# First MLP's down projection: three of its four groups by seven half-tile products per two-by-two block instead of eight

## The reference, cut to what matters

```python
def squared_relu_mlp(x, w1, w2):
    return jnp.square(jax.nn.relu(x @ w1)) @ w2

# in first_block, layer i = 0:
f = squared_relu_mlp(rms_norm(h, pre_mlp_norm[i]), w_mlp_in[i], w_mlp_out[i])
h = h + rms_norm(f, post_mlp_norm[i])
```

## Time and profile before

| quantity | value |
|---|---|
| median of three runs | 2287.64 us |
| span of the profiled execution | 2286.1 us |
| PE busy | 2252.4 us (99% of the span), 10594 matmuls |
| PEld busy | 1848.7 us (81%) |
| POOL busy | 1577.5 us (69%) |
| DVE busy | 1267.0 us (55%) |
| ACT busy | 657.5 us (29%) |
| mean granted clock of PE | 0.997 of full speed |
| DMA | 202.35 MB, mean 89 GB/s |

### The profile page before, as it was taken

How to read it: one execution, slowest core, us unless ns; L and a number is a source line. 1 busy time by engine, 2 the same in 40 slices (tenths; PEclk the granted TensorE clock), 3 DMA queues, 4 the chain that set the end, 5 groups by cost and what they waited for, 6 DMA issues and landing times.

```text
span 2286.1 us, 27986 instructions
## 1 busy us (share of the span) xinstructions
PE 2252.4 (99%) x10594; PEld 1848.7 (81%) x10594; DVE 1267.0 (55%) x1852; ACT 657.5 (29%) x1201; POOL 1577.5 (69%) x1534
## 2 busy tenths in 40 slices
PE   8999999999999999999999999999999999999998
PEld 6888888888888788888888888888677788888887
DVE  7774746335345777175554364368865445626354
ACT  3443432101013455154221011142464233202113
POOL 8666568777777455644597777779445938878784
PEclk9999999999999999999999999999999999999999
DMA  5222233333333111211243333324222413333332
GB/s 168 87 73 85 70 92 92 102 100 98 96 97 89 55 39 40 76 42 53 78 118 108 97 108 104 97 84 142 82 65 70 124 52 97 97 98 97 97 95 77
DMA packets 114264, 202.35 MB, mean 89 GB/s; under 512 B 13009, under 2 KB 21713, under 8 KB 114129
## 3 DMA queue, kind: packets, MB, share of 16 engines
q1 hardware_dynamic: 109424, 194.67, 29.3%
q10 hardware_dynamic: 4704, 5.89, 0.8%
HBM read 196.19 MB, written 2.10 MB: 87 GB/s over the span
## 4 chain that ended last, share of the span: by engine, by line
PE 89%; DVE 5%; POOL 3%; ACT 2%; issue 0%; DMA 0%; SPq 0%; DVEq 0%; POOLq 0%; ACTq 0%
PE bank L499 26%; PE bank L501 26%; PE bank L500 26%; POOL wL L2907 2%; DVE bank L2025 1%; DVE h L2017 1%; PE bank L966 1%; POOL wH L2905 1%; PE bank L548 1%; PE bank L936 1%; PE bank L935 1%; PE bank L937 1%; PE bank L673 1%; PE bank L943 1%; PE bank L944 1%; DVE aL L2025 1%
## 5 line engine op out<-in xcount | busy, mean ns | idle before, releaser
L2907 POOL TENSOR_TENSOR wL<-raw,wH 128x512 fp32r<-128x512 f32 (+2 forms) x732 | 1012.2, 1383 | 61.0
L2905 POOL TENSOR_SCALAR wH<-raw 128x512 fp32r<-128x512 f32 (+2 forms) x732 | 525.9, 718 | 533.1 <-PE bank L501 459.0
L499 PE MATMUL bank<-aH,wH 128*128 128x512 f32 (+2 forms) x1392 | 548.5, 394 | 8.4 <-DVE aL L2025 7.3
L501 PE MATMUL bank<-aH,wL 128*128 128x512 f32 (+2 forms) x1392 | 539.7, 388 | 0.0
L500 PE MATMUL bank<-aL,wH 128*128 128x512 f32 (+2 forms) x1392 | 539.5, 388 | 0.0
L499 PE MATMUL bank<-uH,wH 128*128 128x512 f32 (+1 forms) x1010 | 384.1, 380 | 0.0
L500 PE MATMUL bank<-uL,wH 128*128 128x512 f32 (+1 forms) x1010 | 382.4, 379 | 0.0
L501 PE MATMUL bank<-uH,wL 128*128 128x512 f32 (+1 forms) x1010 | 382.4, 379 | 0.0
L499 PEld LDWEIGHTS bank<-aH,wH 128*128 128x128 f32 (+1 forms) x1392 | 261.8, 188 | 67.5 <-POOL wL L2907 7.2
L500 PEld LDWEIGHTS bank<-aL,wH 128*128 128x128 f32 (+1 forms) x1392 | 261.9, 188 | 55.3 <-issue 3.2
L501 PEld LDWEIGHTS bank<-aH,wL 128*128 128x128 f32 (+1 forms) x1392 | 261.6, 188 | 54.3
(11 more groups left out here) (325 smaller groups left out, 3177.3 us busy)
## 6 DMA issues: line engine op xcount, KB each, us to landing
raw<-in_ws SPq DMA_DIRECT2D x698, 256.0 KB, 2.6
raw<-in_ws SPq DMA_DIRECT2D x24, 192.0 KB, 2.3
d_xr<-F ACTq DMA_DIRECT2D x32, 67.5 KB, 2.8
h<-in_xT SPq DMA_DIRECT2D x8, 256.0 KB, 5.7
E<-in_memT ACTq DMA_DIRECT2D x16, 128.0 KB, 2.7
raw<-in_ws SPq DMA_DIRECT2D x10, 128.0 KB, 2.1
tmp<-in_pT ACTq DMA_DIRECT2D x4, 256.0 KB, 3.2
out<-c_F SPq DMA_DIRECT2D x2, 512.0 KB, 2.8
```

What stands on the lines that cost most here:

```text
L499: P.e.matmul(o, lH, rH, start=start, stop=False, skip_group_check=skip)
L501: return P.e.matmul(o, lL, rH, start=False, stop=stop, skip_group_check=skip)
L2905: G.e.tensor_scalar(H, x, 1.0, 0.0, MUL, ADD).then_inc(*G.did("wH", n))
L2907: G.e.tensor_tensor(L, x, H.bitcast(F32), SUB).then_inc(*G.did("w", n))
```

## The change

The down stage of groups 1, 2 and 3 of the first MLP is computed from two-by-two blocks. A block takes the two output tiles 2m and 2m + 1 against the even and the odd feature tiles 2p and 2p + 1, on the two halves of the tokens. With a11, a21, a12, a22 for the weights (first figure: output tile; second: even or odd features) and b11, b12, b21, b22 for the squared activations (first figure: even or odd features; second: token half) the seven products and the sums they need are

PE's part of the change, and what it waits for:

```diff
+            def seven(i, g, m, ready):
+                for kind in FACTORS:
+                    n, o, c = at, into[kind], COMBO[kind]
+                    P.wait_ge(V if kind in ("s1", "s2", "s4") else G, "w", n)
+                    if kind in ("a11", "s1") and m:
+                        P.wait_ge(V, "R1" if kind == "a11" else "R5", i, g, m - 1)
+                    if kind in ("s2", "a12"):
+                        P.wait_ge(A, "U1", *key)
+                    if kind in ("s3", "s4"):
+                        P.wait_ge(A, "U2", *key)
+                    if kind == "a22":
+                        P.wait_ge(A, "U3", *key)
+                    for p in range(4):
+                        ready(p, c)
+                        x = combo(p, c)
+                        P.e.matmul(o, L[:, p, :], x[:, 0:256], start=first, stop=False, skip_group_check=True)
+                        P.e.matmul(o, H[:, p, :], x[:, 0:256], start=False, stop=False, skip_group_check=True)
+                        j = P.e.matmul(o, H[:, p, :], x[:, 256:512], start=False, stop=p == 3, skip_group_check=True)
...
+                    if i == 0 and g:
+                        four = [take(n, i, g) for n in ("R1", "R5", "R2", "R34")]
+                        for m in range(4):
+                            seven(i, g, m, lambda p, c: P.wait_ge(V, "cL", g, p, C_GROUP[c]))
```

ACT's and DVE's lists for one up tile (`FACTORS` is a11, s1, s2, a12, s3, s4, a22; `C_GROUP` is 0, 0, 1, 1, 2, 3, 3 over the combinations and the products a11, s1 use group 0, s2 group 2, a12 and s4 group 1, s3 and a22 group 3):

```diff
+            def up_seven(g, o):                      # ACT
+                A.wait_ge(V, "r", 0, g, o)
...
+                do(Q[:, 3 if o % 2 else 0, :], bk("up", 0, g, o)[:, :], ACT.Square).then_inc(*A.did("sqr", g, o))
+                for gi in (1, 2, 3) if o % 2 else (0,):
+                    if gi == 1:
+                        A.wait_ge(A, "sqr", g, o)
+                    else:
+                        A.wait_ge(V, ("t5", None, "t6", "t4")[gi], g, p)
+                    do(combos(p, a, b)[:, :, 0:256], c_scratch(Q, gi), ACT.Copy).then_inc(*A.did("cH", g, p, gi))
...
+            def up_seven(g, o):                      # DVE
+                V.wait_ge(P, "up", 0, g, o)
+                stt(x, x, 0.0, root("x", 0), ALU.max, MUL).then_inc(*V.did("r", 0, g, o))
+                V.wait_ge(A, "sqr", g, o)
+                if o % 2 == 0:
+                    tt(Q[:, 1, 0:256], Q[:, 0, 0:256], Q[:, 0, 256:512], SUB).then_inc(*V.did("t5", g, p))
+                    combo_low(g, p, 0)
+                else:
+                    stt(Q[:, 1, 256:512], Q[:, 1, 0:256], -1.0, Q[:, 3, 256:512], MUL, SUB).then_inc(*V.did("t6", g, p))
+                    tt(Q[:, 2, 0:256], Q[:, 3, 256:512], Q[:, 0, 256:512], SUB)
+                    combo_low(g, p, 2)
+                    stt(Q[:, 2, 256:512], Q[:, 1, 256:512], -1.0, Q[:, 3, 0:256], MUL, SUB).then_inc(*V.did("t4", g, p))
+                    combo_low(g, p, 1)
+                    combo_low(g, p, 3)
```

The lists of ACT and DVE around them (`mlp_ple`), and ACT's part of the down stage:

```diff
+                        for o in range(8):           # ACT
+                            up_seven(g, o)
+                            if o == 4:
+                                factor_high(i, g, 0, "a11", "s1")
+                            if o == 5:
+                                factor_high(i, g, 0, "s2", "a12")
+                            if o == 6:
+                                factor_high(i, g, 0, "s3", "s4")
+                            if o == 7:
+                                factor_high(i, g, 0, "a22")
...
+            def down_seven(i, g, m):                 # ACT
+                A.wait_ge(P, "a11", *key)
+                do(R2[:, lo], R1[:, lo], ACT.Copy).then_inc(*A.did("U1", *key))
+                if m < 3:
+                    factor_high(i, g, m + 1, "a11")
+                A.wait_ge(P, "s2", *key)
+                do(R34[:, hi], R2[:, lo], ACT.Copy).then_inc(*A.did("U2", *key))
+                if m < 3:
+                    factor_high(i, g, m + 1, "s1", "s2")
+                A.wait_ge(P, "s3", *key)
+                do(R34[:, lo], R34[:, hi], ACT.Copy).then_inc(*A.did("U3", *key))
+                if m < 3:
+                    factor_high(i, g, m + 1, "a12", "s3", "s4", "a22")
...
+                        for o in range(8):           # DVE
+                            up_seven(g, o)
+                            if o == 4:
+                                factor_sums(i, g, 0, "s1", "s2")
+                            if o == 5:
+                                factor_sums(i, g, 0, "l1", "s4", "l2")
+                            if o == 6:
+                                factor_sums(i, g, 0, "l4")
```

More of the change, by code:

```diff
@@ L43, in plan, with one, seven @@
 def plan():
-    out, behind, spread = [], {}, {}
+    out, slots, behind, spread = [], [], {}, {}
     k8 = tuple(range(8))
+    def one(name, layer, ks, spans):
+        slots.append(("split", len(out)))
+        out.append((name, layer, ks, spans))
     def add(name, layer, ks, spans):
         for ks, spans in pieces(ks, spans):
-            out.append((name, layer, ks, spans))
+            one(name, layer, ks, spans)
+    def seven(name, layer, g, m):
+        at = len(out)
+        for odd, c in ((0, 0), (0, 1), (1, 0), (1, 1)):
+            out.append((name, layer, tuple(8 * g + 2 * p + odd for p in range(4)), cols((128 * (2 * m + c), 128))))
+        for factor in FACTORS:
+            slots.append((factor, at))
     def tile8(name, layer, c0, ks=k8):
@@ L58, in open3 @@
             for name, layer, c0 in keys:
-                out.append((name, layer, half, cols((c0, 128))))
+                one(name, layer, half, cols((c0, 128)))
     def down(name, layer, ks, three):
@@ L86, in mlp_ple @@
         open3(*[("w_mlp_in", layer, 128 * o) for o in range(3)])
-        behind[len(out) + 1] = f"x{layer}"
+        behind[len(slots) + 1] = f"x{layer}"
         for g in range(4):
@@ L102, in mlp_ple @@
         open3(*keys_next)
-        behind[len(out) + 1] = f"n{layer}"
+        behind[len(slots) + 1] = f"n{layer}"
     mlp_ple(0, *[("mla_w_in", 0, 128 * o) for o in (3, 4, 0)])
@@ L182, in plan @@
         down("w_down_2", 0, ks, True)
-    return out, behind, divided, spread
+    return out, slots, behind, divided, spread
 VECS = [
@@ L807, in mlp_ple @@
                 three_run(lin, f"x{i}")
-                three_give(lin, *[(V, "r", i, 0, o) for o in range(3)])
+                up_free = lambda g, o: (A, "sqr", g, o) if i == 0 and g else (V, "r", i, g, o)
+                three_give(lin, *[up_free(0, o) for o in range(3)])
                 for g in range(4):
@@ L1565, in mlp_ple @@
                 for g in range(4):
+                    if i == 0 and g:
+                        for o in range(8):
[8 more added lines that the diff above has]
+                                factor_high(i, g, 0, "a22")
+                            if o in (1, 2, 3) and step < 9:
+                                table_step(i, step)
+                                step += 1
+                        for m in range(4):
+                            down_seven(i, g, m)
+                            if g == 3 and m == 2:
+                                A.wait_ge(P, "up done", i, 3)
+                                p_split(i, 1)
+                            if g == 3:
+                                for o in (2 * m, 2 * m + 1)[0:2 if m < 3 else 1]:
+                                    A.wait_ge(V, "F", "down", i, g, o)
+                                    square(("mlp", i), o, F[:, o, :])
+                        continue
                     if g:
@@ L1592, in mlp_ple @@
                             square(("mlp", i), o, F[:, o, :])
-                for half in range(2):
+                for half in (0, 1) if i else (1, 0):
                     A.wait_ge(V, "F", "down", i, 3, 7, half)
@@ L2310, in into_half, with factor_sums, part @@
                 tt(F[:, 7, c], F[:, 7, c], bk(*event, half)[:, 0:256], ADD).then_inc(*V.did("F", *event, half))
+            def factor_sums(i, g, m, *steps):
+                n1, n2, n4 = (slot_of(i, g, m, kind) for kind in ("s1", "s2", "s4"))
+                r = SLOTS[n1][1]
+                S0, S1 = bk("sum7", 0)[:, :], bk("sum7", 1)[:, :]
+                def part(kind):
+                    V.wait_ge(raw_in[r_ring[r + RAW[kind]]], r + RAW[kind])
+                    return raw_at(r + RAW[kind])
+                for step in steps:
+                    if step == "s1":
+                        if m or g > 1:
+                            V.wait_ge(V, "w", slot_of(*before(i, g, m), "s4"))
+                        a21, a22 = part("a21"), part("a22")
+                        tt(S0, a21, a22, ADD).then_inc(*V.did("s", n1))
+                    elif step == "s2":
+                        a11 = part("a11")
+                        V.wait_ge(V, "s", n1)
+                        tt(S1, S0, a11, ADD).then_inc(*V.did("s", n2))
+                    elif step == "s4":
+                        a12 = part("a12")
+                        V.wait_ge(V, "s", n2)
+                        V.wait_ge(V, "w", n1)
+                        tt(S0, S1, a12, ADD).then_inc(*V.did("s", n4))
```

(26 more changed lines are left out.)

227 lines of the change are left out of this document (196 added, 31 removed).

## The result

The changed kernel takes 2312.89 us (median of 4 runs, 2310.55 to 2315.13), the kernel before, measured beside it, 2288.93 us. The ratio is 1.0106 with a 95% interval of 1.0094 to 1.0118: slower by 24 us. The forecast was 2321 us with a range of 2298 to 2341.

What follows compares the result with a forecast made beforehand. PE was taken as the bound, busy 2252.4 of 2286.1 us. Terms -10.1 + 27.2 + 13.8 + 0.4 + 2.0 = +33.3 us gave 2319.4, or 2321 us timed, range 2298 to 2341.

Steps and rivals of the forecast that it cites:

- The saving: Down stages of groups 1 to 3: 336 half-tile matmuls at 0.1198 us take 40.25 us per group, 10.1 us less altogether.
- The stall at a11: PE waits at block 0's first product for DVE's low part of up tile 6: 9.9, 9.9 and 7.4 us, sum 27.2.
- the exclusion: Up stages: POOL's subtractions hold up DVE's two-operand SBUF operations, 0.49 us for each of 20, 9.8 us per group.
- the table: Angle table steps in DVE's up-stage list: 7.3 us for three steps, 4.8 us for group 3's two.
- The stall at s2: PE waits for U1, ACT's first copy between banks: 6.4 us chain against 1.8 us of PE work, 13.8 us in three groups.
- My floor for a DVE that is never late: At s2 with no lock cost: a 5.1 us chain against 2.9 us of PE work leaves 2.2 us per group.
- Inside the down stage: Blocks after the seam: DVE, ACT and POOL fit within a block's 10.1 us of PE work, so no cost.
- The clock: Long PE waits lower the granted clock behind them: 2 us taken, bounds 0 and 7 us.
- The tail: Behind the down stage: one more 256-column addition before the norm, 0.4 us.
- the signs: Expected: three 7 to 10 us gaps released by DVE, three of 4 to 5 by ACT, none inside blocks 1 to 3.
- only the seam: Rival: the lock costs nothing, stalls of 0.1 and 3 x 2.2 us remain, 2285 us, no change; chance 0.09.
- faster: Rival: DVE stands 2 us ahead, a11 never waits, U1 under 1 us late per group, 2280 us; chance 0.09.

Runs made afterwards that it cites:

- eight-edit kernel: Six edits' kernel, plus U3 ahead of block 1's s1 and s2 high parts, R5 and R1 additions ahead of l1, s4, l2: 2280.64 us, ratio 0.9966.
- the table's experiment: Changed kernel with the angle table's eight steps moved behind group 0's down tiles: 2302.02 us, ratio 1.0062 to the kernel before.
- the second experiment: Changed kernel with group 3's square of tile 2m - 1 behind U2 in ACT's list: 2305.14 us, ratio 1.0074 to the kernel before.
- kernel with six edits: Three edits' kernel, plus s4's low part behind last up tile, s2's high part not awaiting s4, square behind s1 and s2 high parts: 2284.18 us.
- kernel with three edits: Changed kernel with table in group 0, group 3's squares behind U2, U1 of block 0 early: 2294.19 us, ratio 1.0030 to the kernel before.

## Why the prediction came out right

**The saving** of 10.1 us was right: the eight-edit kernel saves 9.9 in the three stages, at the pitch that the earlier trace rows gave. The 109 ns for 256 columns that the Trainium skill ("TensorE: Matmul & The Clock Gate", section "Back-to-back issue gap") gives as the isolated gap is not what this stream shows: 336 of them took 40.00 us, 119 ns each.

**The stall at a11** had its place and cause right and its size wrong: 27.2 us forecast, 10.9 measured. Three terms were too large. First, the exclusion: I gave 9.8 us per group. The 24 operations in group 1's rows lose 9 x 0.05 + 6 x 0.36 + 6 x 0.10 + 3 x 0.15 = 3.7 us against 0.69 and 0.42 us undisturbed. In groups 2 and 3 the same 24 lose 6.3 and 7.1 us; the nine full-size ones alone lose 2.5 us, here of group 2:

```profile
L2224 DVE TENSOR_TENSOR u<-Q,u 128x512 fp32r<-128x512 f32 x9 | 8.6, 963 | 2.4 <-ACT u L1491 2.2
```

The sum s1 adds 1.1 us in each group (1.80 us instead of 0.69). So the exclusion was overdrawn by half in group 1 and by much less in the others, and how much an operation loses depends on where it falls among POOL's. Second, an operation of 256 columns: I took 0.42 to 0.48 plus a gap, but such operations follow each other at 0.35 us (464.63, 464.98 in the changed kernel). Third, the table: 5.8 us in group 1, not 7.3. Left alone by POOL's subtractions its steps take 3.5 us, so they too were held up, by 2.3 us here and by 3.8 in the kernel before. My rule named operations with two operands from SBUF only, and was too narrow.

**The stall at s2** was 8.3 us, not 13.8: the chain takes 5.5 us instead of 6.4, and in groups 2 and 3 PE's own work beside it ran at the lower clock, 3.1 and 3.0 us instead of 1.9. At full clock the three waits would be 3.57 us each, 10.7 together (an estimate from group 1's). That it doesn't need the wait at a11 is shown by the table's experiment (3.5 us). My floor for a DVE that is never late, 2.2 us, fits: with DVE's lateness at tile 7 taken off, 1.6 us there and 1.1, 1.1 and 0.6 us without POOL's low parts, 1.9 us is left each time (an estimate; no run has U1 in its place and DVE on time).

**Inside the down stage** I forecast nothing, and this step failed: 6.9 us in group 3. My count of ACT's work in a block left out the squares for the norm, which only group 3 has, and above all their place. The busy time fitted (26.3 of 56.6 us); what counted was the one instruction that waits for DVE and stands ahead of U1. I had named gaps in blocks as a sign that I was wrong, and here they are.

**The clock** cost 7.8 us, more than the upper bound of 7 and not the 2 I took. 2.4 us of it are hidden in the chain to U1, as I had reasoned that a part would be. The number and length of the waits alone don't say what it costs: with waits of 1.56 and 3.57 us group 3 stayed at 1.00 in the second experiment, with one of 3.52 us group 1 fell to 0.96 in the first. What decides it stays open. **The tail** cost nothing: the 192 matmuls behind the stage take 44.9 us before and after.

So the sum of +33 against +23.9 in the stages was near in part by luck: two oversized stalls (by 16.3 and 5.5 us) and two undersized terms (6.9 and 5.8 us) partly cancelled. Of the signs, the six places at the seams and what releases them came true, their sizes did not (2.3 to 5.0 us instead of 4 to 10).

Of the rivals, "only the seam" gave 2285 us, and the kernel with six edits takes 2284.18, but by other waits than that rival's, so it has not come true. In "faster", the gaps that I named add up to 4 x 0.14 + 3 x 0.07 = 0.8 us per group, not the 2 us by which DVE was to stand ahead.

## What to carry to other kernels

Saving work on the bounding engine by a cleverer product is worth what the preparing engines can still hide at the seam: add up the dependent chain from the last input to the first operand, and place every hand-over copy in its engine's list ahead of work that waits for something else. An engine busy for less than half of the time (ACT, 26.3 of 56.6 us) can still stop the bounding one through a single in-order wait, so look in such a list for what stands ahead of the hand-over, not at busy shares. Clear waits one after the other and take the trace anew each time, since the waits at a22 and the short ones in blocks 0 and 1 only showed when those before them were gone.

## What the runs showed of the hardware

The same wait does not always bring the clock down. With POOL's low parts left out, s2 waits 3.01 us in group 1 and 3.02 us in group 2; the granted clock of the stage is 0.93 in the first and 1.00 in the second:

```profile
470.17:515.99 45.82, 42.97 (x338) 42.76 (x337) 26.97 (x46) 19.04 (x40) 26.49 (x23) 0.93 0.27 84
559.54:602.64 43.10, 40.24 (x338) 40.03 (x336) 27.00 (x46) 18.95 (x40) 26.54 (x23) 1.00 0.29 88
```

The difference is 2.7 us, nearly as much as the wait itself. The kernel with three edits shows it again: waits of 1.24 and 2.09 us in group 1 and a clock of 0.96, waits of 1.29 and 2.12 us in group 2 and a clock of 1.00. No run here shows what makes the difference.

POOL's subtractions hold up not only DVE's operations on two SBUF operands. With them left out, the table's CAST of one 128 x 512 operand took 0.41 us instead of 1.51.
